# Two steps of projections in every second round of the triangular solver, in place of one step in each of four rounds

## What is computed

```
m = jnp.where(tri_strict, jnp.einsum('bhnid,bhnjd->bhnij', k_beta, k) * decay, 0.0)
sol = lax.linalg.triangular_solve(eye + m, rhs, left_side=True, lower=True, unit_diagonal=True)
```

```
proj = hn @ w_in[layer]
```

## Time and profile before

| what | value |
|---|---|
| time, median of 3 runs | 1982.76 us (1979.36 to 1983.71) |
| the profiled execution's own time | 1983.47 us |
| its span | 1981.3 us |
| mean granted TensorE clock | 0.996 of full |
| TensorE matmul (PE) busy | 1915.3 us, 97% |
| TensorE weight load (PEld) busy | 1686.6 us, 85% |
| VectorE, ScalarE, GpSimd busy | 391.4, 285.4, 89.8 us |

### The profile page before, as it was taken

One profiled execution on the slowest core, in us unless ns is written; L12 is line 12 of the kernel. 1 busy time (PEld: TensorE's weight loads), 2 busy tenths in 40 slices (PEclk: granted clock), 3 DMA queues, 4 the chain that ended last, 5 costly groups with the idle time before them and its releaser, 6 DMA issues.

```text
span 1981.3 us, 68659 instructions
## 1 busy us (share of the span) xinstructions
PE 1915.3 (97%) x31758; PEld 1686.6 (85%) x31758; DVE 391.4 (20%) x942; ACT 285.4 (14%) x612; POOL 89.8 (5%) x174
## 2 busy tenths in 40 slices
PE   7999999999999999999999899999999999999998
PEld 7888788887778688878888799989999899999997
DVE  3445331110000234633211201010010101010101
ACT  1323332010000122332310100000000000000001
POOL 4011100000000001011100000000000000000000
PEclk9999999999999999999999899999999999999999
DMA  8422223476433051412346699999999999999996
GB/s 248 128 65 88 64 86 113 139 262 202 160 122 107 23 170 46 127 45 65 107 147 217 224 354 414 407 411 417 407 416 406 418 411 416 411 416 415 414 414 247
DMA packets 183535, 483.03 MB, mean 244 GB/s; under 512 B 13118, under 2 KB 111628, under 8 KB 183436
## 3 DMA queue, kind: packets, MB, share of 16 engines
q1 hardware_dynamic: 183436, 481.55, 64.6%
HBM read 480.46 MB, written 1.05 MB: 243 GB/s over the span
## 4 chain that ended last, share of the span: by engine, by line
PE 88%; DMA 6%; DVE 3%; ACT 1%; issue 1%; SPq 0%; POOL 0%; DVEq 0%; ACTq 0%
PE bank L647 37%; PE bank L634 19%; PE bank L1181 7%; DMA pool<-in_moe_w_down_dram 6%; PE bank L1104 4%; PE bank L1141 4%; PE bank L746 3%; PE bank L1120 3%; PE bank L695 2%; PE bank L1307 1%; PE bank L739 1%; PE bank L1067 1%; DVE pool L1832 1%; PE bank L1027 0%; PE bank L1004 0%
## 5 line engine op out<-in xcount | busy, mean ns | idle before, releaser
L647 PE MATMUL bank<-pool 128*64 128x80 f32 x21504 | 765.6, 233 | 26.8 <-DMA pool<-in_moe_w_down_dram 18.7
L647 PEld LDWEIGHTS bank<-pool 128*64 128x64 f32 x21504 | 751.4, 137 | 42.4 <-DMA pool<-in_moe_w_down_dram 21.5
L634 PE MATMUL bank<-hnT,pool 128*128 128x256 f32 x1856 | 427.1, 383 | 0.5 <-DVE pool L1894 0.4
L634 PEld LDWEIGHTS bank<-hnT,pool 128*128 128x128 f32 x1856 | 345.4, 190 | 55.3 <-issue 9.3
L2061 DVE TENSOR_TENSOR pool<-pool,bank 128x320 f32<-128x320 f32 x64 | 27.4, 446 | 670.8 <-PE bank L647 670.8
L1181 PEld LDWEIGHTS bank<-hnT,pool 128*128 128x128 f32 x640 | 121.6, 190 | 23.4 <-issue 7.6
L1181 PE MATMUL bank<-hnT,pool 128*128 128x256 f32 x640 | 140.7, 379 | 0.0
L1600 ACT ACTIVATE pool<-bank 128x320 f32<-128x320 f32 x64 | 25.2, 404 | 540.8 <-PE bank L647 540.8
L574 POOL TENSOR_TENSOR pool<-pool,level_mask 128x256 f32<-128x256 f32 x72 | 53.5, 758 | 742.3 <-DVE pool L1751 489.4
L1104 PE MATMUL bank<-oT,pool 128*128 128x256 f32 x384 | 85.4, 380 | 0.0
L1104 PEld LDWEIGHTS bank<-oT,pool 128*128 128x128 f32 x384 | 72.8, 190 | 10.2 <-issue 0.3
(11 more groups left out here) (321 smaller groups left out, 1205.0 us busy)
## 6 DMA issues: line engine op xcount, KB each, us to landing
pool<-in_moe_w_gate_dram SPq DMA_DIRECT2D x128, 896.0 KB, 13.1
pool<-in_moe_w_up_dram SPq DMA_DIRECT2D x128, 896.0 KB, 8.4
pool<-in_moe_w_down_dram SPq DMA_DIRECT2D x160, 512.0 KB, 7.1
pool<-in_w_in_dram SPq DMA_DIRECT2D x66, 1024.0 KB, 5.4
pool<-in_moe_w_down_dram SPq DMA_DIRECT2D x32, 1024.0 KB, 9.3
pool<-in_ffn_w_gate_dram SPq DMA_DIRECT2D x11, 1024.0 KB, 7.5
pool<-in_ffn_w_up_dram SPq DMA_DIRECT2D x11, 1024.0 KB, 5.5
pool<-in_ffn_w_down_dram SPq DMA_DIRECT2D x11, 1024.0 KB, 5.0
```

Of the source, the lines that this page charges most:

```text
L634: ins = mm(ps[:, s * T:(s + 1) * T], w[:, k, (j + s) * P:(j + s + 1) * P], hnT[:, k, :], start=(k == 0), stop=(k == KD - 1))
L647: ins = mm(bank[rows, cs], w[:, rows], rhs, start=start, stop=stop, skip_group_check=True)
```

## The change

The solver takes two steps where it took one, and the rounds that open with steps are 2 and 4 and no longer 2, 3, 4 and 5. The number of steps within a solver stays four.

```diff
@@ -755,7 +755,7 @@
                     x0_mm.by(ins)
                 for b in range(1, 6):
                     if b in share:
-                        some(steps, 1)
+                        some(steps, 2)
                     for g in range(2):
@@ -845,7 +845,7 @@
-                solver(l, 0, steps, (2, 3, 4, 5))
+                solver(l, 0, steps, (2, 4))
@@ -968,7 +968,7 @@
-                    solver(l, 1 + q, steps, (2, 3, 4, 5))
+                    solver(l, 1 + q, steps, (2, 4))
```

## The result

The changed kernel takes 1997.94 us (median of 4 runs, 1995.06 to 2003.70) against 1982.53 us before (median of 4 runs, one more than in the table above, 1979.36 to 1983.71); the ratio is 1.0082, 95% interval 1.0061 to 1.0103. It is slower by about 16 us, where no difference was forecast and the range ended at 1985.3 us. Of all runs of this case a single one was in the slow state, one of the kernel before at 4594.35 us beside the last three timed kernels, and it is left out everywhere. The profiled execution took 2003.7 us, its span is 2001.5 us, its mean granted clock 0.987 (before: 0.996).

What follows compares the result with a forecast made beforehand. TensorE, busy 97% of the span, was taken as the bound. A pair of rounds went from 1.22 + 1.22 to 0.36 + 2.08, both 2.44 us, so no difference: 1982.8 us, range 1979.3 to 1985.3 us.

Steps and rivals of the forecast that it cites:

- The bounds now: TensorE is busy 97% of the span; a microsecond a solver gains or loses there moves the end by about one.
- The double step: Two steps opening a solver round take 1.92 us from first record to y pass, each further step costing 0.87 us.
- The bare gap: In rounds opening without a step, the y pass starts 0.36 us (0.31 to 0.46) behind the last x records.
- the wake: TensorE's start after a VectorE signal in a bare round, taken as 0.05 to 0.06 us; one row showed 0.15 us.
- Half 1 and GpSimd: In bare rounds, VectorE's half 1 is ready in time, margin under 0.1 us; GpSimd stays covered with 0.8 us to spare.
- What else moves: Some solver steps come one round earlier, touching weight slots, PSUM banks and freed loads; all costed at nothing.
- The clock rival: Bare rounds' short idle pauses drop TensorE's clock to 1.2 GHz: up to 29 us more, about 2012 us; chance 0.02.
- The clock leaves 1.00 within a solver: Sign that the prediction is wrong: the granted clock, 1.00 (2.4 GHz) through all of a solver before, falls there.
- the sum: Each pair of solver rounds stays at 2.44 us; over 12 pairs no difference, bounds -0.6 to +1.2 us.

Runs made afterwards that it cites:

- run 1: Not an experiment: one of a layer's three solver runs. Changing only this and run 2 against the kernel before (four of six solvers) measured 1.0056.
- run 2: Not an experiment: one of a layer's three solver runs. Changing only this and run 1 against the kernel before (four of six solvers) measured 1.0056.
- load-late kernel: Changed kernel with SyncE holding back the weight load that a step inside a solver frees until that solver's last x pass is done; 1983.65 us, ratio 1.0009.
- the repeated comparison: Unchanged copy of the changed kernel, timed once more against the kernel before; ratio 1.0076 (1.0051 to 1.0101).
- the first four kernels: Copies of the kernel before (1.0002) and changed kernel (1.0076), and the change only in the solver of run 0 (0.9995) or of run 1 and run 2 (1.0056).
- run 0: Not an experiment: one of a layer's three solver runs. Changing only its solver against the kernel before (two of six solvers) measured 0.9995.

## Why the prediction was wrong

Point by point, in the order of its steps.

- **The bounds now, and that TensorE's time in a solver counts fully:** nothing speaks against it. What the solvers lost and the end lost agree to about 1 us in the account below.
- **The double step, 1.92 us:** right to the hundredth.
- **The bare gap, 0.36 us:** the term was mis-sized by the wake. It measured 0.46 us, the upper bound. I had two rows for the wake and took the one with the same signal (0.06 us) over the one with the same waiting instruction (0.15 us, a y pass); the latter was the nearer relation. Price: +1.2 us instead of 0. The waits for VectorE line 1675 grew with it from 1.6 to 4.2 us, a little above the 3 to 4 us forecast.
- **Half 1 and GpSimd:** right, no y pass waits for either.
- **"What else moves", costed at nothing:** this step failed. It treated the freed load as something that TensorE waits for or does not. It looked at when the load is issued (the same round, right for run 1) and when its weights are needed, and never at what the load delays. The runs showed that TensorE's own instruction fetches can come out behind it, at 245.56 and 878.69 us in the changed kernel, 4.5 and 4.7 us behind the issue of the load. The 2.6 and 2.9 us pauses follow such fetches: moving the load alone took them away (1.0076 to 1.0009), and shifting the steps moved them. The pauses and the falls of the clock at them make up most of the 15 us that the sum lacks. The sentence on run 2, that the load one round earlier "is not waited for in the solver", names the very event that made the first pause.
- **The clock rival, 0.02:** it had the consequence right and the mechanism wrong. The short waits of 0.23 us were not what told: with all twelve of them left in and the load held back, the mean clock of the runs was 0.9938 against 0.9945 beside them. With the pauses it was 0.9898 against 0.9946. The kernel's own pauses of nearly 3 us, which that rival did not see, come with falls in three of four places in the two profiles. Over all profiles there are eight pauses of over 1.5 us in the solvers (1.54 to 2.91 us), and at seven of them the clock goes down, from 0.6 us before TensorE resumes to 1.5 us after. In the six profiles without bare rounds no fall lies within a solver. The one fall in a solver with bare rounds and no long pause, in the load-late kernel, leaves room for a small share of that rival. "The clock leaves 1.00 within a solver" was one of the prediction's own signs of being wrong, and it came.

The account of the repeated comparison (medians 1994.29 and 1979.42 us, 14.9 us apart): lost clock is (1 - 0.9898) x 1994 = 20.3 us against (1 - 0.9946) x 1979 = 10.7 us, so 9.6 us more. Pauses are 5.5 us less the 0.5 to 0.7 us that before has, and the bare gaps 1.2 us, together 6.0 to 6.2 us. The sum is 15.7 us against 14.9 measured. The clock's part is an estimate that takes all lost clock for lost time, and the pauses are those of one profile of each kernel; that all the additional lost clock follows from the pauses is shown only as far as it vanished, to 1.4 us, when the pauses were taken away.

One sign was readable in the profile of before. In run 2 of layer 0 it had a pause of 0.47 us in the middle of a y pass with no releaser but issue, right behind a weight load:

```profile
246.40 1.15 PE L746 MATMUL bank<-pool 64*64 64x64 f32 x31 [0.47 <-issue]
```

The prediction did not use this row. With the runs at hand it reads as a fetch that came half a microsecond too late, number 23, at 243.93 us, behind the load of 239.18 us. So the margin there was gone already, and number 22 had come only 1.2 us ahead of that load. It is also the one that the hold removed in the kernel before.

## What to carry to other kernels

- Where a stretch is made of many tiny matmuls, it uses up instructions fastest: in the kernel before, the instruction packets are mostly 3.4 to 5.9 us apart in the solvers, and 17.5 and 25.7 us apart between 129.80 and 173.04 us, where 128x256 matmuls prevail. Look there for idle time by issue inside a group, and at the instruction queue in the DMA view. A large load issued in such a stretch can starve the engine although nobody waits for the load.
- If a step frees a slot, moving it moves a DMA. Ask not only who needs that transfer but what it gets in front of.
- For the wake behind a wait, take the price from a row in which the same instruction waits; and don't leave an unexplained half microsecond on the path unplaced.

## What the hardware showed that was not expected

- Fetches of TensorE's instructions come in packets of 16 KB, one every 4 us or so in the solvers. Behind a 1 MB load one came 8.7 us after the one before (870.0 to 878.7 us in the profile of the changed kernel). All 15 idle times by issue of over 0.65 us in the solvers had a load issued 3.4 to 4.9 us ahead of the packet. Without any load since the packet before, nine of 0.31 to 0.62 us are on record.
- The clock falls ahead of any changed instruction in some executions of either kernel and not in others (80 us: yes in one profile of before, no in the other; the same for the changed kernel). Of the 20 us between the first two profiles this fall alone makes 3.4 us. Ratios over many runs were needed; the 27 runs of before beside the first four kernels alone scatter from 1976.73 to 1987.63 us.
- Changes that touch neither a pause nor the work, such as the load held back in the kernel before, moved the mean clock by 0.0024 and the time by 5 us. This stays open.
